# Two attention stages: values as the stationary operand in two column halves, probabilities divided on GpSimd, and one maximum over two banks

## The chip, the cores and the metric

The kernel runs on one core of a Trainium2 chip, as one launch. The metric is the time on the device in microseconds (us), the median over several runs. A core has TensorE (PE; its weight loads are PEld), VectorE (DVE), ScalarE (ACT), GpSimd (POOL) and the DMA queue of SyncE (SP). They run at the same time and wait for each other only through semaphores.

## The reference

The reference is a small language model block of three mixers over 512 tokens of width 1024, in fp32. The first is a hybrid layer. The second and third are a forgetting attention ("fox") and a latent attention ("mla"), each with 12 heads of 64, beside 4 heads that look at a memory of 256 tokens, and each followed by an output projection and a convolutional feed-forward block. What the change touches is the softmax attention of the second and third:

```python
logits = jnp.einsum('bhqd,bhkd->bhqk', qc, k).astype(jnp.float32)
if log_decay is not None:
    logits = logits + args[2][..., None] - log_decay[:, :, None, :]
logits = jnp.where(key_idx[None, :] <= q_idx[:, None], logits, -jnp.inf)
p = jax.nn.softmax(logits, axis=-1).astype(v.dtype)
return jnp.einsum('bhqk,bhkd->bhqd', p, v)
...
x = x + jnp.concatenate([o_mix, o_mem], axis=-1) @ w_out[i]
```

`log_decay` is there in forgetting attention only. The attention is causal, over query blocks of 128, so a head's block i has 128 (i + 1) keys. The memory heads have all 256 keys for every block and no mask.

## The kernel before

One list, `SCHEDULE` (made by `schedule()`, line 2893), fixes the order of all work. It names a stage for each step, and every engine's program walks through the same list; the engine's generator for that stage then issues what belongs to that step. So each engine's order is written by hand and served strictly in order; waits go by named events (`Signal`, `Waits`). Buffers come from rings: `take` waits until the last holder of the buffer was released. PSUM is 8 banks of 128 x 512 fp32.

The dense products (projections, feed-forward) split each fp32 factor into a high part and a rest, both of the type fp32r, and sum three products (`mm3`, lines 320 to 323). Weights come by DMA into `wstage`; ScalarE makes the high part (L302) and VectorE the rest (L312), in pieces set between the other steps.

Both attention stages use the class `Attention` and the generators `pe_att`, `act_att` and `dve_att` (lines 989 to 1222), as does the first mixer's banded attention. An item is one head and one block of 128 queries; with 16 heads there are 64 items in a mixer. Items come in pairs of heads. In forgetting attention the two heads of a pair alternate and their scores are made together, one head in each half of the array's rows (64 channels each); `fox_order` (L2230) sets a group of memory items between them. In latent attention a head has 96 channels, and a head's four blocks come one after another. At step t:

- TensorE makes the scores of item t (L1051 to L1068) in a bank, transposes the probabilities of item t - 3 (L1077), block by block of 128 keys, and multiplies those of item t - 5 with the values (L1092). There the transposed probabilities are the stationary operand (128 x 128) and the 64 columns of the values stream. The result is queries by channels, in a bank for both heads of a pair.
- VectorE takes the negated maximum of item t - 1 (L1182), and copies the transposed probabilities of item t - 3 out of their bank (L465), except those of forgetting attention's memory heads, which ScalarE copies (L460).
- ScalarE makes the exponential with the sum of its row (L1140). In latent attention it first multiplies the maximum by the query's norm, a column of 128 (L1138).
- Five and six steps after a pair's last item VectorE takes the reciprocals of the 8 sums (L1191) and multiplies the outputs of each block (L1197, four for a pair) into `y`. TensorE then transposes `y`, four blocks (L1108), and ScalarE and VectorE split the result into `hhi` and `hlo` (L418, L427), the operand of the output projection.

The output projection's first tile (`pe_out`, step 0) runs between the last steps of attention. In latent attention the projections of the heads to come (`pe_group`, `act_group`, `dve_group`, `pool_group`) share the first 43 steps.

```python
for t in A.steps:                       # pe_att, L1095
    if 0 <= t < N and A.scored(t) and not late:
        score(A.scored(t))
    if 3 <= t <= N + 2:
        turn(t - 3)
    if 5 <= t <= N + 4:
        pv(t - 5)
```

## Time and profile before

| what | value |
|---|---|
| median of 3 runs | 1573.14 us (1569.53 to 1573.67) |
| time of the profiled execution | 1568.96 us |
| span of the profiled execution | 1567.2 us |
| TensorE busy | 1532.4 us, 98% |
| VectorE busy | 824.6 us, 53% |
| ScalarE busy | 723.4 us, 46% |
| GpSimd busy | 317.8 us, 20% |
| mean granted TensorE clock | 0.998 |

The span goes from the first to the last instruction; the time of the execution is 1.8 us more. "Busy" counts an engine as busy while any of its instructions runs. The instructions of one engine overlap (a matmul's duration includes the time until its result has landed), so a count times a mean duration is more than the busy time, and what one instruction costs in a dense stretch is the distance between two starts.

### The profile page before, as it was taken

How to read it: one execution, taken by the hardware profiler on the slowest of the kernel's cores; microseconds unless marked ns; L12 is line 12 of the kernel's file. 1: busy time of each engine (PE TensorE's matmuls, PEld its weight loads, DVE VectorE, ACT ScalarE, POOL GpSimd, SP SyncE). 2: the span in 40 equal slices, each digit the busy share in tenths (PEclk: the TensorE clock that was granted, in tenths of full speed). 3: DMA queues.
4: the chain of work that ended last, by engine and by line, in shares of the span. 5: the costliest groups of instructions: out<-in, count | busy, mean ns of one | idle time of the engine just before them, and what ended most of it. 6: DMA issues, size and time to landing. Idle time of an engine off the chain costs nothing. (4 is left out here: it accounts for less than half of the span.)

```text
span 1567.2 us, 22136 instructions
## 1 busy us (share of the span) xinstructions
PE 1532.4 (98%) x9018; PEld 1288.9 (82%) x9018; DVE 824.6 (53%) x1405; ACT 723.4 (46%) x1402; POOL 317.8 (20%) x270
## 2 busy tenths in 40 slices
PE   7999998999999999999999999999999999999999
PEld 6888887998898887888888888668887888888887
DVE  5346556556435755745234443668956544244442
ACT  4346545455654544544124443567844443134431
POOL 0000142001430001344013431032001433024420
PEclk9999999999999999999999999999999999999999
DMA  6212112323220103233223332110022333223331
GB/s 234 75 41 88 54 55 89 129 68 108 78 89 27 39 1 108 82 107 119 90 79 102 100 111 75 48 44 14 16 66 81 105 97 122 80 81 98 114 111 41
DMA packets 37462, 128.07 MB, mean 82 GB/s; under 512 B 4192, under 2 KB 8944, under 8 KB 37360
## 3 DMA queue, kind: packets, MB, share of 16 engines
q1 hardware_dynamic: 37360, 126.65, 24.9%
q8 instruction: 71, 1.16, 0.3%
q14 instruction: 31, 0.25, 0.1%
HBM read 124.54 MB, written 2.10 MB: 81 GB/s over the span
## 5 line engine op out<-in xcount | busy, mean ns | idle before, releaser
L321 PE MATMUL bank<-hhi,whi 128*128 128x512 f32 (+2 forms) x1064 | 418.3, 393 | 2.8 <-ACT hhi L1936 1.8
L323 PE MATMUL bank<-hhi,wlo 128*128 128x512 f32 (+2 forms) x1064 | 414.4, 390 | 0.0
L322 PE MATMUL bank<-hlo,whi 128*128 128x512 f32 (+2 forms) x1064 | 414.2, 389 | 0.0
L312 DVE TENSOR_TENSOR wlo<-wstage,whi 128x1024 fp32r<-128x1024 f32 (+9 forms) x250 | 278.6, 1117 | 112.2 <-ACT whi L302 111.8
L302 ACT CAST whi<-wstage 128x1024 fp32r<-128x1024 f32 (+9 forms) x250 | 236.1, 949 | 135.6 <-PE bank L323 131.7
L2421 DVE SCALAR_TENSOR_TENSOR cr<-bank,vc,cr 128x511 f32<-128x511 f32 (+1 forms) x168 | 125.9, 749 | 217.1 <-ACT cr L2360 214.1
L321 PEld LDWEIGHTS bank<-hhi,whi 128*128 128x128 f32 (+2 forms) x1064 | 198.7, 187 | 49.3 <-ACT hhi L1936 4.3
L323 PEld LDWEIGHTS bank<-hhi,wlo 128*128 128x128 f32 (+2 forms) x1064 | 198.6, 187 | 43.2
L322 PEld LDWEIGHTS bank<-hlo,whi 128*128 128x128 f32 (+2 forms) x1064 | 198.7, 187 | 41.7 <-issue 0.5
L2360 ACT ACTIVATE cr<-bank,vc 128x512 f32<-128x512 f32 x84 | 65.5, 780 | 248.5 <-PE bank L323 246.1
L2466 POOL TENSOR_TENSOR cr<-cr,cr 128x512 f32<-128x512 f32 x44 | 94.4, 2146 | 315.4 <-DVE cr L2421 280.7
L321 PE MATMUL bank<-ahi,whi 128*128 128x512 f32 x352 | 137.8, 392 | 1.7 <-POOL alo L2472 1.7
L323 PE MATMUL bank<-ahi,wlo 128*128 128x512 f32 x352 | 137.1, 389 | 0.0
L322 PE MATMUL bank<-alo,whi 128*128 128x512 f32 x352 | 137.0, 389 | 0.0
L2472 POOL TENSOR_TENSOR alo<-cr,ahi 128x512 fp32r<-128x512 f32 x44 | 95.6, 2172 | 118.9 <-ACT ahi L2372 118.8
L321 PE MATMUL bank<-whi,hhi 128*128 128x384 f32 (+3 forms) x288 | 96.8, 336 | 1.5 <-issue 0.9
L322 PE MATMUL bank<-wlo,hhi 128*128 128x384 f32 (+3 forms) x288 | 94.1, 327 | 1.7 <-issue 1.7
L2445 DVE TENSOR_TENSOR xT<-bank,xT 128x512 f32<-128x512 f32 x32 | 22.1, 691 | 137.1 <-PE bank L323 137.1
L323 PE MATMUL bank<-whi,hlo 128*128 128x384 f32 (+3 forms) x288 | 94.1, 327 | 0.0
L321 PEld LDWEIGHTS bank<-ahi,whi 128*128 128x128 f32 x352 | 66.1, 188 | 16.7 <-issue 3.3
L323 PEld LDWEIGHTS bank<-ahi,wlo 128*128 128x128 f32 x352 | 66.1, 188 | 13.9
L322 PEld LDWEIGHTS bank<-alo,whi 128*128 128x128 f32 x352 | 66.1, 188 | 13.4
(412 smaller groups left out, 2298.5 us busy)
## 6 DMA issues: line engine op xcount, KB each, us to landing
wstage<-in_wts SPq DMA_DIRECT2D x147, 512.0 KB, 3.5
wstage<-in_wts SPq DMA_DIRECT2D x32, 704.0 KB, 4.0
wstage<-in_wts SPq DMA_DIRECT2D x14, 768.0 KB, 4.3
xT<-in_x SPq DMA_DIRECT2D x4, 512.0 KB, 5.3
xt<-in_x SPq DMA_DIRECT2D x4, 512.0 KB, 5.9
out<-ob SPq DMA_DIRECT2D x8, 256.0 KB, 2.3
U<-in_rel_ext SPq DMA_DIRECT2D x6, 256.0 KB, 9.0
wstage<-in_wts SPq DMA_DIRECT2D x2, 603.0 KB, 3.9
```

The source lines that it names most:

```text
L302: e.copy(K.whi[i % 3][:, p], K.stage[i % 3][:, p]).then_inc(*K.act.up(("whi", i, p.stop)))
L312: e.tensor_tensor(K.wlo[i % 3][:, p], K.stage[i % 3][:, p], K.whi[i % 3][:, p].bitcast(F32), SUB).then_inc(*K.dve.up(("wlo", i) if last el ...
L321: e.matmul(o, lh, rh, start=start, stop=False)
L322: e.matmul(o, lh, rl, start=False, stop=False)
L323: return e.matmul(o, ll, rh, start=False, stop=stop)
L2360: e.activation(t[:], divided(K, 1 + 2 * l, key) if first else K.bank(key)[:], ACT.Identity, scale=K.col(f"cw{l}", 3 * ch + 2), bias=K.col( ...
L2421: e.scalar_tensor_tensor(out=t[:, s:T], in0=b[:, 0:T - s], scalar=K.col(f"cw{l}", 3 * ch + 2 - s), in1=t[:, s:T], op0=MUL, op1=ADD).then_i ...
L2445: e.tensor_tensor(K.xT[:, m, :], K.bank((down, hv, m))[:], K.xT[:, m, :], ADD).then_inc(*K.dve.up(done, frees=[(down, hv, m)]))
L2466: e.tensor_tensor(g[:], g[:], v[:], MUL).then_inc(*K.pool.up(("gated", l, ch), frees=[((up, 22 + ch), "cr")]))
L2472: e.tensor_tensor(alo[:, ct, :], g[:], ahi[:, ct, :].bitcast(F32), SUB).then_inc(*K.pool.up(("alo", l, hv, ct), frees=[((up, 11 * hv + ct) ...
```

## The change

The first mixer keeps `pe_att`, `act_att` and `dve_att`, with their branches for the others removed. The other two get a subclass and generators of their own:

- The transposed probabilities are the streaming operand and the values (128 keys x 64 channels) the stationary one. The result comes out as channels by queries, the first head of a pair in partitions 0 to 63 and the second in 64 to 127 of one bank; `values(p, i)` issues the products of both heads for a block, alternating.
- The division by the sums comes before the transpose. For every two items VectorE takes the reciprocals (2 columns), and GpSimd multiplies the probabilities by them, in place, one instruction an item.
- `y`, its divisions (L1197) and its transposes (L1108) are gone; `hhi` and `hlo` are made from the bank of the products.
- The transpose of item t comes at step t + 5, the products of a block 7 steps after its second item; there are 7 buffers for probabilities in place of 5, and one buffer a head and block for the transposed ones.
- In forgetting attention one `tensor_reduce` takes the maxima of two items, from two adjacent banks (banks 0 to 3 are now one tensor).
- In latent attention the product of maximum and norm is GpSimd's.
- Banks are dealt out anew, and the steps of the schedule's lists change by one or two.

```diff
+class TurnedAttention(Attention):
+    TURN, VALUES = 5, 7
...
+def pe_turned(e, q, K, A):
...
     def turn(t):
         n = A.n(t)
         b = A.T.take(q, (A.name, "T", t))
-        q.wait_ge(*K.at((A.name, "P", t)))
+        q.wait_ge(*K.at((A.name, "divided", t)))
...
+    def values(p, i):
+        if i == 0:
+            (A.O4 if p < 2 else A.O).take(q, (A.name, "O", p))
+        for t, item in enumerate(A.items):
+            if item in ((2 * p, i), (2 * p + 1, i)):
+                q.wait_ge(*K.at((A.name, "pt", t)))
+        n = A.blocks(2 * p, i)
+        z = {}
+        for j in range(n):
...
+            for s in range(2):
+                o = K.bank((A.name, "O", p))[64 * s:64 * s + 64, i * P:(i + 1) * P]
+                z[s] = e.matmul(o, A.heads[2 * p + s].v(j), A.turned(p, i)[s][:, j, :], start=j == 0, stop=j == n - 1)
...
     for t in A.steps:
         late = 0 <= t < N and A.R is not None and A.items[t][0] >= 4
         if 0 <= t < N and A.scored(t) and not late:
             score(A.scored(t))
-        if 3 <= t <= N + 2:
-            turn(t - 3)
-        if 5 <= t <= N + 4:
-            pv(t - 5)
...
+        if t - A.VALUES in A.ends:
+            values(*A.ends[t - A.VALUES])
+        if 0 <= t - A.TURN < N:
+            turn(t - A.TURN)
...
+def act_turned(e, q, K, A):
...
-            e.activation(m, m, ACT.Identity, scale=factor).then_inc(*K.act.up((A.name, "mx", t)))
...
+        p = A.done(t - A.VALUES - 1)
         if p is not None:
             kt = (p + 6) % 8
-            act_hi(e, q, K, (A.gen, "hi", kt), (A.name, "yT", p), K.hhi[:, kt, :])
+            for i in range(4):
+                q.wait_ge(*K.at((A.name, "pv", p, i)))
+            e.copy(K.hhi[:, kt, :], K.bank((A.name, "O", p))[:]).then_inc(*K.act.up((A.gen, "hi", kt)))
...
+def dve_turned(e, q, K, A):
...
+    def soft_two(t):
+        h, i = A.items[t]
+        n, m = A.n(t), A.mx[:, h:h + 2, i]
+        q.wait_ge(*K.at((A.name, "S", t)))
+        q.wait_ge(*K.at((A.name, "S", t + 1)))
+        e.tensor_reduce(m, K.both[t % 4][:, :, 0:n], AX, MAX, negate=True).then_inc(*K.dve.up((A.name, "mx", t), (A.name, "mx", t + 1)))
...
+        u = t - 3
+        if 0 <= u < N and u % 2 == 0:
+            q.wait_ge(*K.at((A.name, "P", u)))
+            q.wait_ge(*K.at((A.name, "P", u + 1)))
+            e.reciprocal(A.sums(u), A.sums(u)).then_inc(*K.dve.up((A.name, "rr", u)))
...
+def pool_turned(e, q, K, A):
+    N = len(A.items)
+    for t in A.steps:
+        u = t - 1
+        if 0 <= u < N and A.heads[A.items[u][0]].factor:
...
+            e.tensor_tensor(m, m, factor, MUL).then_inc(*K.pool.up((A.name, "mx", u)))
+        u = t - 3
+        if 0 <= u < N and u % 2 == 0:
+            q.wait_ge(*K.at((A.name, "rr", u)))
+            for item in (u, u + 1):
+                h, i = A.items[item]
+                p = A.P[A.name, "P", item][:, 0:A.n(item)]
+                e.tensor_scalar(p, p, A.rs[:, h, i:i + 1], None, MUL).then_inc(*K.pool.up((A.name, "divided", item)))
...
-    out += ["fox", "foxatt", "foxatt"] * 5 + ["foxatt"] * 61
-    out += ["out0"] + ["foxatt"] * 3 + ["out0"] * 7 + ["bar5"] + ["norm1"] * 2 + ["ffn0"] * 63 + ["bar6"] + ["norm2"] * 2
+    out += ["fox", "foxatt", "foxatt"] * 5 + ["foxatt"] * 60
+    out += ["out0"] + ["foxatt"] * 5 + ["out0"] * 7 + ["bar5"] + ["norm1"] * 2 + ["ffn0"] * 63 + ["bar6"] + ["norm2"] * 2
```

## Rows read from the trace of the kernel before

**Rows 1.** The page: the span, and part 1, busy time of each engine.
```profile
span 1567.2 us, 22136 instructions
...
PE 1532.4 (98%) x9018; PEld 1288.9 (82%) x9018; DVE 824.6 (53%) x1405; ACT 723.4 (46%) x1402; POOL 317.8 (20%) x270
```

**Rows 2.** Windows: length, busy (instructions) of PE, PEld, DVE, ACT, POOL; clock; DMA.
```profile
484.00:573.00 89.00, 87.66 (x828) 76.78 (x827) 61.58 (x166) 48.67 (x161) 0.00 (x0) 1.00 0.06 19
1028.00:1066.00 38.00, 34.36 (x217) 27.19 (x216) 27.65 (x73) 28.22 (x91) 17.16 (x23) 0.96 0.12 36
1066.00:1151.00 85.00, 81.70 (x668) 73.82 (x667) 73.11 (x178) 67.36 (x196) 7.78 (x10) 1.00 0.08 26
```

**Rows 3.** Lines with each shape apart, TensorE, 482 to 574 us: busy, mean | idle.
```profile
L1092 PE MATMUL bank<-fv,fox_pt 128*128 128x64 f32 x240 | 31.9, 265 | 0.0
...
L1092 PE MATMUL bank<-vmem,fox_pta 128*128 128x64 f32 x64 | 8.9, 262 | 0.0
...
L1108 PE MATMUL bank<-ident,y 128*128 128x128 f32 x28 | 4.4, 279 | 0.3 <-DVE y L1197 0.3
```

**Rows 4.** The same view, TensorE, 1028 to 1154 us.
```profile
L1092 PE MATMUL bank<-vt,mla_pt 128*128 128x64 f32 x240 | 31.9, 265 | 0.0
...
L1092 PE MATMUL bank<-vmem,mla_pt 128*128 128x64 f32 x64 | 9.4, 271 | 2.0 <-DVE y L1197 2.0
```

**Rows 5.** Timeline, TensorE, 566 to 582 us: start, length, engine, line, count.
```profile
570.25 2.57 PE L1092 MATMUL bank<-fv,fox_pt 128*128 128x64 f32 x22
```

**Rows 6.** Lines with each shape apart, TensorE, the whole span: fp32 products of two widths.
```profile
L1884 PE MATMUL bank<-tmp,ones 128*128 128x512 f32 x6 | 3.1, 592 | 0.0
...
L2009 PE MATMUL bank<-tmp,blk 128*128 128x256 f32 x4 | 1.0, 380 | 0.0
```

**Rows 7.** Timelines, TensorE, from 540.1 and from 243.7 us: row halves, column strips.
```profile
540.20 0.70 PE L1051 MATMUL bank<-kmg,mqT 64*128 64x256 f32 x4
...
243.71 0.34 PE L1503 MATMUL bank<-gq,gk 32*32 32x32 f32 x32
```

**Rows 8.** Timeline, TensorE, 541 to 546.5 us.
```profile
541.61 0.60 PE L1077 MATMUL bank<-ident,tmp 128*128 128x128 f32 x4
...
543.27 0.23 PE L1068 MATMUL bank<-later,below 64*128 64x64 bf16 x4
543.43 0.66 PE L1077 MATMUL bank<-ident,tmp 128*128 128x128 f32 x4
...
544.77 1.00 PE L1092 MATMUL bank<-fv,fox_pt 128*128 128x64 f32 x8
545.70 0.39 PE L1051 MATMUL bank<-fkh,fqh 64*128 64x256 f32 x2
```

**Rows 9.** Lines with each shape apart, VectorE, 482 to 574 us.
```profile
L1182 DVE TENSOR_REDUCE fox_mx<-bank 128x1 f32<-128x512 f32 x12 | 8.2, 680 | 0.6 <-PE bank L1068 0.6
L1197 DVE TENSOR_TENSOR y<-bank,fox_rs 128x128 f32<-128x128 f32 x32 | 7.6, 282 | 0.3
...
L1182 DVE TENSOR_REDUCE fox_mx<-bank 128x1 f32<-128x128 f32 x12 | 3.0, 281 | 1.5 <-PE bank L1068 1.5
L1191 DVE RECIPROCAL fox_rs<-fox_rs 128x8 f32<-128x8 f32 x8 | 1.6, 202 | 13.1 <-PE bank L1092 13.1
```

**Rows 10.** Lines, ScalarE: one row of 1028 to 1154 us, two of 482 to 574.
```profile
L1138 ACT ACTIVATE mla_mx<-mla_mx,r 128x1 f32<-128x1 f32 x48 | 14.0, 292 | 14.3 <-DVE mla_mx L1182 14.2
...
L1140 ACT ACTIVATION_READ_ACCUMULATOR tmp<-bank,fox_mx 128x1 f32 x64 | 12.5, 196 | 0.0
L1140 ACT ACTIVATE tmp<-bank,fox_mx 128x512 f32<-128x512 f32 x12 | 8.3, 688 | 3.8 <-DVE fox_mx L1182 3.8
```

**Rows 11.** Lines with each shape apart, GpSimd, the whole span.
```profile
L2472 POOL TENSOR_TENSOR alo<-cr,ahi 128x512 fp32r<-128x512 f32 x44 | 95.6, 2172 | 118.9 <-ACT ahi L2372 118.8
...
L1871 POOL TENSOR_TENSOR sum<-sum,tmp 128x512 f32<-128x512 f32 x10 | 13.0, 1300 | 41.3 <-ACT tmp L1835 41.3
...
L2822 POOL COPY kt<-krr 128x512 f32<-128x512 f32 x3 | 1.8, 611 | 51.3 <-DVE krr L2703 51.2
```

More of the change, by code:

```diff
@@ L1042, in pe_att, with turned_to @@
+def turned_to(A, q, K, t):
+    h, i = A.items[t]
+    if A.before[h // 2, i] is not None:
+        q.wait_ge(*K.at((A.name, "pv", *A.before[h // 2, i])))
+    else:
+        for event in A.free_after:
+            q.wait_ge(*K.at(event))
+    n = A.blocks(h, i)
+    return A.turned(h // 2, i)[h % 2], K.bank((A.name, "T", t))[:, 0:n * P].rearrange("p (j n) -> p j n", j=n)
 def pe_att(e, q, K, A):
@@ L1047, in score @@
+def pe_turned(e, q, K, A):
+    N = len(A.items)
+    def score(ts):
+        at = [(t, A.items[t][1], A.heads[A.items[t][0]], A.n(t), A.scores(t).take(q, (A.name, "S", t))) for t in ts]
         z = {}
@@ L2853, in pool_group @@
             *K.pool.up(("k", j, "normed", h)))
-    yield
-    for _ in range(3):
         yield
```

313 lines of the change are left out of this document (194 added, 119 removed).

## The prediction

> **What bounds the kernel now.** I began with the page: TensorE is busy for 98% of the span and no other engine for more than 53% [rows 1]. So time goes only where TensorE's work shrinks, or where TensorE waits. Then I cut out the two stages that the change touches, by the windows view [rows 2]. In forgetting attention (484 to 573 us) TensorE is idle for 1.3 of 89 us, and VectorE is busy for 61.6. Latent attention has an early part that shares its time with the projections of its heads (1028 to 1066), and a late part (1066 to 1151) in which TensorE is idle for 3.3 of 85 us and VectorE busy for 73.1. So the first stage is TensorE's alone; in the second VectorE stands close behind. GpSimd does nothing in the first stage and 7.8 us in the late part of the second.
>
> **TensorE, the products with the values.** An fp32 product is two passes in the trace: 120 blocks of 128 by 128 show as 240, and each mixer has 240 + 64 = 304 passes [rows 3, 4]. A run of 22 passes lasts 2.57 us with its last 0.275 [rows 5], so they start 2.295/21 = 0.109 us apart. That is not the 64 columns that stream: a pass of 512 columns takes 0.592 us and one of 256 takes 0.380 [rows 6], 0.83 ns a column, so 64 columns are 0.05 us. What fills 0.109 us is the load of 128 columns of weights. After the change a pass loads 64 columns and streams 128: 128 x 0.83 = 0.106 us, with a load of half the width (about 0.05) that the earlier pass can cover. One pass is thus hardly cheaper. The gain hangs on the two heads running side by side in the two column halves. Two rows speak for it. The memory heads' scores use two row halves, and their four passes of 256 columns fit in 0.70 us [rows 7], where four in turn would need four times 256 x 0.83 = 0.85 us before any load. For columns, 32 passes of 32 by 32 run in 0.34 us, the last 0.19 of it, so all start within 0.15 us [rows 7]; with four row strips alone, one strip would stream eight passes of 32 x 0.83 = 0.027 us, 0.21 us. Passes in one strip but different column strips must have overlapped, and in fp32. So I take full overlap: 152 passes' time of 0.106 per mixer, 16.1 us, in place of 304 x 0.109 = 33.1. That is -17.0 per mixer. The bound on the other side is no overlap, 32.2 us.
>
> The Trainium skill (TensorE: Matmul & The Clock Gate, section "Measured speedup vs the span model") reports 2.38 for three column tiles, not 3. At that efficiency (0.79) the products would take an estimated 20.4 us a mixer and the sum would be 8.6 us smaller; no row here has halves of 64 columns.
>
> **TensorE, the rest.** The transposes of y go: 32 per mixer (28 before 574 us) [rows 3]; four of their size start (0.60 - 0.27)/3 = 0.11 us apart [rows 8], so -3.5 per mixer. A change of tile shape costs: the last product before a score starts at 544.77 + 1.00 - 0.275 = 545.50, the score at 545.70 [rows 8], 0.20 in place of 0.11; the way back (543.27 to 543.43) loses as much. I take 0.1 a change. In forgetting attention the order score, transpose, product becomes score, product, transpose, three changes in place of two for each of 32 calls of values(); in latent attention the scores span 96 rows and needed none, so each call adds two. With 0.05 for a first load in each call: +4.8 and +8.0. TensorE's sum: -17.0 - 3.5 + 4.8 = -15.7 in forgetting, -17.0 - 3.5 + 8.0 = -12.5 in latent attention. Of the latter the late part has 240 of 304 passes and 24 of 32 calls: -10.0; the early part -2.5.
>
> **VectorE.** The 32 divisions of y go, 0.282 each, 9.0 us; reciprocals go from 8 to 32 at 0.20, +4.8 [rows 9]. A maximum costs 0.281 for 128 and 0.680 for 512 columns [rows 9], so 0.15 fixed; 32 double ones in place of 64 save 4.8. (Never shown is one over two banks: from no saving to 0.15 each.) Busy in forgetting attention: 61.6 - 9.0 + 4.8 - 4.8 = 52.6, of a stage that TensorE needs 89 - 15.7 = 73.3 for: 72%, nearly its share now, so TensorE keeps its gain. In the late part of latent attention: 73.1 - 24 x 0.282 + 18 x 0.20 = 69.9, against TensorE's 85 - 10.0 = 75.0, or 93%, where it is 86% now. An engine that serves in order can't be that full without being waited for; I take 92%, 76 us, a gain of 9. In the early part the projections' norms set the pace (VectorE 27.7, ScalarE 28.2 and GpSimd 17.2 busy of 38): gain 1.
>
> **ScalarE** loses 48 scalings of 0.29 us, 14.0 us [rows 10], to GpSimd, which does them in the same chain (maximum, scaling, exponential): nothing saved on latency. It is not the bound; 0.
>
> **GpSimd** gets 128 divisions. Per mixer these are 6 pairs x 2 heads x 1280 columns + 16 x 256 = 19,456, or 38 full widths. The trace has none with one input and a scalar per row. Ends: a copy of 512 takes 0.611; a two-input operation 1.30, or 2.17 in the feed-forward stage [rows 11]. I take 0.65, next to the one-input row: 25 us a mixer, hidden beside TensorE, as 1.30 (49 us) would be too. What the division does add is length: the transpose comes at step t+5, not t+3. From the end of a 512-wide score pair: double maximum 1.2, two exponentials 0.69 each with their accumulator reads [rows 10], reciprocal 0.2, division 0.65; some 4 us against five steps of TensorE, 5 us. That holds in mid-stage. At the end nothing follows the last items, so transpose 62 waits about 2 us before the output projection's first tile; it then covers the last one. -2 for each mixer. The single output bank is freed by ScalarE's and VectorE's parts of y three or more steps before its next use, as a memory group stands between pairs: 0.
>
> **Sum.** Forgetting 15.7 - 2 = 13.7; latent 9 + 1 - 2 = 8; together 22. Against the profiled execution's 1568.96 us that is 1547. The median of the runs is 4.2 us higher, so 1551.
>
> **Rivals.** (1) VectorE keeps up all the same: TensorE's sum counts whole, 15.7 + 12.5 = 28, giving 1545. For: VectorE's buffers are several steps deep. Against: 93%. (2) GpSimd becomes the bound. At the feed-forward stage's 2.17 us a width, forgetting attention needs 38 x 2.17 = 82 us of it (gain 7) and the late part 30 x 2.17 + 7.8 + 48 small scalings of up to 0.29, 87 us, no gain: 1566. For: the same operation costs 1.30 or 2.17 by where it runs. Against: it has one input here, and VectorE's work beside it reads mostly the banks. The Trainium skill (GPSIMD Engine Reference, Specifications) says that the shared SBUF interfaces clash when VectorE has two SBUF inputs; by that rule forgetting attention, where only the weights' splits do, is free, and no run so far shows the divisions. (3) Slower: the halves take turns. Place: values(). If the loads stay hidden the products cost 64.4 in place of 66.3, -1.9, less 7.0 for y, plus 12.8 for changes and loads: +4. If a load can't pass the other half's stream, 608 x 0.05 = 30 more. So +4 to +34, 1577 to 1607, with 1590 as its time. It decides once a pass costs on average over 0.10 us (66.3 + 7.0 - 12.8 = 60.5 over 608), where I expect 0.053. Against it the 32 by 32 row; for it, both halves stream all 128 rows, which that row doesn't. (4) The edit does less than it says: probabilities arrive so late that TensorE's saved time becomes waiting for "divided" at each wide pair, 1 us x 12 in each mixer: 1573, no change.
>
> **Chances.** Forecast 0.60, (1) 0.13, (2) 0.10, (3) 0.12, (4) 0.05. A change of under 0.3% (4.7 us) can't be told from none here. Faster by more: 0.60 + 0.13 + most of (2), 0.82. Within: (4) and the top of (2), 0.06. Slower: 0.12. The range runs from just below (1), if the double maximum and the end chains cost nothing (1537), to (2) and the edge of (4), 1572; it leaves out (3) and half of (4).
>
> **What the changed profile would show.** Products of 128*64 with 128x128 in pairs that start within some ns, their pairs 0.11 us apart; forgetting attention about 75 us, the late part about 76; TensorE's idle there rising to some 5 us, put down to VectorE's copies or maxima; VectorE above 90%; divisions near 0.65 us. Wrong if the second half's passes start 0.1 us after the first's, if TensorE's waits name the division, or if GpSimd is busy for over half of a stage.

## The result, and the profile after

The change makes the kernel slower. Its median is 1614.16 us over 4 runs (1613.33 to 1619.62), beside 1571.34 us (1565.97 to 1573.67) for the kernel before: a ratio of 1.0285 with a 95% interval of 1.0248 to 1.0322. I had forecast 1551 us and a range up to 1572. The profiled execution took 1613.33 us, 44.4 more than that of before.

The page, the span and part 1:

```profile
span 1611.6 us, 22131 instructions
...
PE 1537.0 (95%) x8954; PEld 1264.4 (78%) x8954; DVE 816.8 (51%) x1357; ACT 706.9 (44%) x1354; POOL 458.1 (28%) x446
```

Beside [rows 1]: TensorE's busy time has not fallen at all, though it has less to do; GpSimd has 140.3 us more; VectorE and ScalarE have 7.8 and 16.5 less. To see where the 44.4 us lie I cut the span where both traces have the same event: the forgetting part runs from VectorE's first maximum to ScalarE's first activation of the feed-forward block, the latent part from the last activation of that block to the first of the next. These two rows, from the view of one tile (the feed-forward's, ScalarE), the first of before and the second of after, give one of these edges:

```profile
L2360 ACT ACTIVATE cr<-xd,vc x2: 802/808/815, 637.4 to 638.1; 128x512 f32<-128x512 f32 x2
```
```profile
L2529 ACT ACTIVATE cr<-xd,vc x2: 798/808/817, 651.7 to 652.4; 128x512 f32<-128x512 f32 x2
```

The first maximum starts at 482.2 and 482.3 us, so the forgetting part takes 155.2 us before and 169.4 after. The latent part takes 293.1 and 323.2. The feed-forward block between them (285.1) and all behind them (351.6) are the same within 0.1, here and in every run below. So +14.2 and +30.1, with 0.1 in the start, make the 44.4. The table holds these two lengths for all runs, as I read them off each trace, and beside each how long TensorE was granted the lower of its two clock levels in it (1.2 GHz; otherwise 2.4). Single runs are marked; their time stands for itself, without an interval. Ratios compare runs in the faster of two states; one of e18's four runs, at 1738.57 us, fell in the slower one and is left out.

| kernel | us | forgetting (half clock) | latent (half clock) |
|---|---|---|---|
| before | 1571 to 1573 | 155.2 (0) | 293.1 (3.4) |
| after | 1614.16 | 169.4 (13.7) | 323.2 (41.0) |
| e1_no_division, one run | 1586.75 | 155.5 (0) | 307.7 (27.3) |
| e2_half_columns, one run | 1600.53 | 163.2 (13.7) | 314.0 (41.0) |
| e3_vector_divides, one run | 1602.58 | 158.2 (3.4) | 319.9 (41.0) |
| e4_shared, one run | 1597.65 | 157.4 (3.4) | 317.5 (41.0) |
| e6_two_maxima_alone | 1573.14 | 157.2 (0) | 292.7 (3.4) |
| e14_scaling_alone | 1569.83 | 155.2 (0) | 292.2 (0) |
| e15_forgetting_alone, one run | 1584.82 | 171.6 (23.9) | 293.2 (3.4) |
| e7_scaling_on_scalar | 1610.67 | 170.8 (23.9) | 316.0 (34.1) |
| e9_single_maxima_scalar_scaling, one run | 1588.33 | 157.6 (6.8) | 309.5 (30.7) |
| e10_short, one run | 1578.07 | 148.6 (0) | 304.2 (23.9) |
| e11_filled, one run | 1611.62 | 167.1 (0) | 321.3 (27.3) |
| e12_fill_light, one run | 1568.46 | 148.6 (0) | 300.1 (10.2) |
| e13_even_values, one run | 1579.99 | 150.1 (3.4) | 305.0 (0) |
| e18_changed_filled_light | 1617.00 | 172.8 (27.3) | 321.4 (27.3) |
| e19_copies_on_scalar | 1574.02 | 155.2 (0) | 294.1 (3.4) |
| e20_filled_copies_on_scalar, one run | 1578.8 | 150.2 (3.4) | 305.2 (20.5) |
| e17_forgetting_shared | 1589.18 | 175.6 (30.7) | 291.8 (0) |

Some of this scatters without a change of code. The first maximum starts between 480.7 and 489.0 us over these profiles, though the work ahead of it is the same, and the ten runs of e6 spread over 8.9 us. So totals of single runs can't be compared to a few us; the parts are steadier. The latent attention of before stands in four profiles (before, e6, e15, e17) with 291.8 to 293.2 us. The forgetting attention of the changed kernel stands in four as well (after, e7, e15, e18) with 169.4, 170.8, 171.6 and 172.8, in the order of their time at half clock (13.7, 23.9, 23.9, 27.3).

The windows of the changed kernel: forgetting attention, its end beside the output projection's first tile, and latent attention's early and late part. The columns are those of [rows 2]:

```profile
482.00:575.00 93.00, 77.43 (x756) 55.42 (x756) 53.44 (x125) 44.64 (x159) 60.52 (x60) 0.96 0.06 18
575.00:592.00 17.00, 12.74 (x77) 9.54 (x75) 4.84 (x10) 1.93 (x5) 5.56 (x4) 0.80 0.00 0
1037.00:1075.00 38.00, 30.95 (x184) 21.72 (x183) 25.69 (x75) 26.77 (x88) 26.27 (x32) 0.95 0.15 46
1075.00:1187.00 112.00, 92.11 (x651) 71.98 (x649) 73.46 (x178) 58.41 (x162) 70.30 (x110) 0.86 0.05 15
```

TensorE now stands idle for 15.6 of 93 us and for 19.9 of 112, and works at a granted clock of 0.96 and 0.86. No engine is full: GpSimd, the busiest newcomer, reaches 65% and 63%. That is the picture of a chain of waits, not of a bound. The waits of 484 to 586 us and, in the second fence, of 1075 to 1187 us (who waited for whom, us in total, times, longest) name its links:

```profile
POOL tmp L1390 <- DVE fox_rs L1365: 45.6, 21, 22.0
DVE fox_pt L465 <- PE bank L1247: 24.7, 27, 3.0
...
PE bank L1247 <- POOL tmp L1390: 9.4, 7, 2.1
...
PE bank L1247 <- POOL fox_p L1390: 3.1, 2, 1.8
```
```profile
ACT tmp L1300 <- POOL mla_mx L1383: 34.7, 19, 3.3
...
ACT mla_p L1300 <- POOL mla_mx L1383: 15.1, 6, 5.5
...
PE bank L1247 <- POOL tmp L1390: 6.0, 7, 1.5
```

TensorE's transposes (L1247) wait for the division (L1390), the second of the three signs that I had named for a wrong forecast; GpSimd at 65% of the stage is the third. In latent attention ScalarE waits 49.8 us for the scaled maximum (L1383), which GpSimd serves in the same queue as the divisions.

### The profile page after: what moved, and what is told of

It reads as the page before. It is cut to its first block and busy times, and to the rows that moved or that the text cites. A ratio compares the mean times of both kernels' runs of the same rounds, so it can differ in the third digit from the quotient of the medians.

```text
span 1611.6 us, 22131 instructions
## 1 busy us (share of the span) xinstructions
PE 1537.0 (95%) x8954; PEld 1264.4 (78%) x8954; DVE 816.8 (51%) x1357; ACT 706.9 (44%) x1354; POOL 458.1 (28%) x446
## 5 line engine op out<-in xcount | busy, mean ns | idle before, releaser
L321 PE MATMUL bank0to<-hhi,whi 128*128 128x512 f32 x560 | 221.5, 396 | 2.8 <-ACT hhi L2105 1.8
L322 PE MATMUL bank0to<-hlo,whi 128*128 128x512 f32 x560 | 219.5, 392 | 0.0
L323 PE MATMUL bank0to<-hhi,wlo 128*128 128x512 f32 x560 | 219.3, 392 | 0.0
L321 PE MATMUL bank<-hhi,whi 128*128 128x512 f32 (+2 forms) x504 | 199.2, 395 | 0.0
L323 PE MATMUL bank<-hhi,wlo 128*128 128x512 f32 (+2 forms) x504 | 196.8, 391 | 0.0
L322 PE MATMUL bank<-hlo,whi 128*128 128x512 f32 (+2 forms) x504 | 196.7, 390 | 0.0
L321 PEld LDWEIGHTS bank0to<-hhi,whi 128*128 128x128 f32 x560 | 106.2, 190 | 28.5 <-ACT hhi L2105 4.2
L323 PEld LDWEIGHTS bank0to<-hhi,wlo 128*128 128x128 f32 x560 | 106.0, 189 | 22.5
L322 PEld LDWEIGHTS bank0to<-hlo,whi 128*128 128x128 f32 x560 | 106.1, 190 | 21.4
L323 PEld LDWEIGHTS bank<-hhi,wlo 128*128 128x128 f32 (+2 forms) x504 | 93.8, 186 | 21.4
```

Source lines behind the costliest of these rows:

```text
L321: e.matmul(o, lh, rh, start=start, stop=False)
L322: e.matmul(o, lh, rl, start=False, stop=False)
L323: return e.matmul(o, ll, rh, start=False, stop=stop)
```

## What the operations cost

The lines of GpSimd with each shape apart, 482 to 620 us, and behind them one row of the same view of ScalarE's old work, now GpSimd's (930 to 1200 us):

```profile
L1390 POOL TENSOR_SCALAR tmp<-tmp,fox_rs 128x256 f32<-128x256 f32 x19 | 17.4, 923 | 28.5 <-DVE fox_rs L1365 28.2
L1390 POOL TENSOR_SCALAR tmp<-tmp,fox_rs 128x512 f32<-128x512 f32 x10 | 15.5, 1563 | 2.3 <-DVE fox_rs L1365 2.3
L1390 POOL TENSOR_SCALAR tmp<-tmp,fox_rs 128x384 f32<-128x384 f32 x8 | 9.9, 1243 | 5.9 <-DVE fox_rs L1365 5.9
...
L1390 POOL TENSOR_SCALAR tmp<-tmp,fox_rs 128x128 f32<-128x128 f32 x9 | 5.3, 603 | 9.2 <-DVE fox_rs L1365 9.2
```
```profile
L1383 POOL TENSOR_TENSOR mla_mx<-mla_mx,r 128x1 f32<-128x1 f32 x48 | 8.7, 189 | 13.5 <-DVE mla_mx L1333 12.4 <-ACT mla_p L1300 1.0
```

A division costs 283 ns and 2.5 ns a column, so 1.563 us for 512 columns, where I had taken 0.65. (In latent attention the rows of the 512-wide ones average 1.59 and 1.66.) A mixer has 12 of each width and 16 more of 256: 12 x (0.603 + 0.923 + 1.243 + 1.563) + 16 x 0.923 = 66.8 us, where I had 25. The Trainium skill (GPSIMD Engine Reference, section 3.1) gives 1.8 cycles an element at 1.2 GHz as the best case of a tight loop, 0.77 us for 512, and about 2.6 for two inputs; these rows show 2.5 ns a column, which at that clock would be three cycles, for one input and a scalar per row. The measurement decides.

TensorE's own part came as forecast. Timeline of TensorE, 515 to 592 us:

```profile
524.80 1.09 PE L1265 MATMUL bank<-fox_pt,fv 128*64 128x128 f32 x16
...
538.63 1.55 PE L1265 MATMUL bank<-fox_pt,fv 128*64 128x128 f32 x12
...
588.73 0.88 PE L1265 MATMUL bank<-fox_pt,fv 128*64 128x128 f32 x12
```

Sixteen passes, eight in each column half, last 1.09 us. The single starts are 524.801 and 524.807, 524.961 and 524.967, then 525.070 and 525.077, and so on by 0.109: the halves run side by side, and a pair costs what one pass did [rows 5]. The middle row is the same work as the last, at half clock: 1.55 in place of 0.88 us.

## Where the chain comes from

One pair of 512 columns can be followed through the timeline of all engines, 559 to 568 us of the changed kernel:

```profile
559.30 0.23 PE L1238 MATMUL bank0to<-later,below 64*128 64x64 bf16 x4
...
560.62 1.22 DVE L1343 TENSOR_REDUCE fox_mx<-bank0to 128x2 f32<-128x1024 f32 x1
...
561.87 0.69 ACT L1300 ACTIVATE tmp<-bank0to,fox_mx 128x512 f32<-128x512 f32 x1 [1.75 <-DVE fox_mx L1343]
...
562.34 2.46 POOL L1390 TENSOR_SCALAR tmp<-tmp,fox_rs 128x384 f32<-128x384 f32 x2 [1.82 <-DVE fox_rs L1365]
...
562.55 0.68 ACT L1300 ACTIVATE tmp<-bank0to,fox_mx 128x512 f32<-128x512 f32 x1
...
563.73 0.52 PE L1247 MATMUL bank<-ident,tmp 128*128 128x128 f32 x3 [1.76 <-POOL tmp L1390]
...
564.28 0.56 DVE L465 COPY fox_pt<-bank 128x384 f32<-128x384 f32 x1 [1.12 <-PE bank L1247]
...
564.76 0.16 DVE L1365 RECIPROCAL fox_rs<-fox_rs 128x2 f32<-128x2 f32 x1
...
565.01 3.10 POOL L1390 TENSOR_SCALAR tmp<-tmp,fox_rs 128x512 f32<-128x512 f32 x2 [0.21 <-DVE fox_rs L1365]
```

The pair's scores end at 559.53, its maximum starts at 560.62, its exponentials end at 563.32 with their sums, and its second division ends at 568.11: 8.6 us, where I had "some 4 us". Three things make it long. The maximum starts 1.1 us after the scores, behind other work of VectorE. Both items' divisions count, 3.10 us, and I had counted one of 0.65. And 1.7 us pass between the sums and the first division. The reciprocal, ready to go at 563.32, starts at 564.76, because on VectorE it stands behind a copy that waits for TensorE's transpose of the pair before, which at 563.73 had waited 1.76 us for that pair's division on GpSimd. GpSimd itself is busy with that pair until 562.34 + 2.46 = 564.80, so for this pair a prompt reciprocal would have brought only 0.21 us; before the 384-wide divisions it was GpSimd that waited, 1.82 us. So the delay goes round: division, transpose, copy, reciprocal, next division, and GpSimd's own queue is a part of it.

## Experiments: the division

Two theories stood first: that the divisions make the loss, by their price and their place in the chain, or that the rest of the new order does (the longer pipeline, the places of the products, the clock), so that free divisions would not help. In e1 the divisions are left out and TensorE waits for the reciprocal in their place; the output is undivided.

```diff
-                e.tensor_scalar(p, p, A.rs[:, h, i:i + 1], None, MUL).then_inc(*K.pool.up((A.name, "divided", item)))
...
-        q.wait_ge(*K.at((A.name, "divided", t)))
+        q.wait_ge(*K.at((A.name, "rr", t - t % 2)))
```

> The changed kernel without GpSimd's 128 divisions; the transpose waits for the reciprocals in their place, so the result is left undivided, and all else stays. Theory A (GpSimd's division is the bound: 283 ns + 2.5 ns a column in the changed trace, 67 us a mixer): the time falls from 1614 to 1540 to 1555 us, the clock stays at 0.99 or more. Theory B (the longer way from score to transpose, two steps and a wait for pairs, costs by itself): it stays above 1580. Theory C (the column halves or the changes of shape cost): stays above 1590.

In e2 only the first half of each item's columns is divided.

```diff
-                p = A.P[A.name, "P", item][:, 0:A.n(item)]
+                p = A.P[A.name, "P", item][:, 0:A.n(item) // 2]
```

> The changed kernel with GpSimd dividing only the first half of each item's columns (the other half is left undivided). Theory A as throughput: GpSimd needs 64 x 0.28 + 9728 x 0.0025 = 42 us a mixer in place of 67, below TensorE's 73, so most of the loss goes: 1550 to 1575 us. Theory A as latency in the chain: about half of the way between the changed kernel and the one without divisions. Theory B or C: little change, above 1590.

Without divisions the two parts shrink by 13.9 and 15.5 us, 29.4 of the 44.3 lost; with half the columns by 6.2 and 9.2, 15.4, about half of that. e1's 1586.75 us lie far above theory A's 1540 to 1555 and within theory B's. In e2 the fixed 283 ns of a division stay, so GpSimd's divisions fall by over a third only, from 66.8 to an estimated 42.4 us, and yet the two parts gain 52% of what they gain without any division. e2's 1600.53 us lie about halfway between the changed kernel and e1, as I had put for a chain of waits, and not at 1550 to 1575, as I had put for throughput. So the cost follows the length of the division, though not in proportion to it. The divisions are two thirds of the loss; the rest, 0.3 us in forgetting and 14.6 in latent attention, is there without any division.

e3 gives all divisions to VectorE; e4 gives the first item of each two to VectorE and leaves the second to GpSimd.

```diff
             e.reciprocal(A.sums(u), A.sums(u)).then_inc(*K.dve.up((A.name, "rr", u)))
+            q.wait_ge(*K.at((A.name, "rr", u)))
+            for item in (u, u + 1):
...
+                e.tensor_scalar(p, p, A.rs[:, h, i:i + 1], None, MUL).then_inc(*K.dve.up((A.name, "divided", item)))
```

> The changed kernel with all 128 divisions on VectorE, behind its reciprocals. Theory A: forgetting attention gains (VectorE has room there), latent attention is bound by VectorE; 1560 to 1590 us in sum, depending on the price of a 512-wide division on VectorE, which no run has shown (0.3 to 0.7 us). Theory B: no gain over the changed kernel, about 1610.

> The changed kernel with the first item of each two divided by VectorE and the second by GpSimd. Theory A: GpSimd falls to 33 us a mixer and VectorE rises by 10 to 22; 1550 to 1575 us, below the kernel before if VectorE's part is short. Theory B: about 1600.

A row of each, the lines with each shape apart (VectorE in e3, GpSimd in e4, 482 to 600 us):

```profile
L1370 DVE TENSOR_SCALAR tmp<-tmp,fox_rs 128x512 f32<-128x512 f32 x10 | 4.5, 483 | 0.2
```
```profile
L1395 POOL TENSOR_SCALAR tmp<-tmp,fox_rs 128x512 f32<-128x512 f32 x5 | 9.3, 1861 | 4.9 <-DVE fox_rs L1365 4.9
```

VectorE divides 512 columns in 0.483 us, a third of GpSimd's time. It recovers 11.2 us of forgetting attention's 14.2, and only 3.3 of latent attention's 30.1; why so little there, no run shows. Shared is the lowest of the three (157.4 and 317.5). GpSimd needs 0.09, 0.16, 0.23 and 0.30 us more for 128 to 512 columns in it: each of its divisions starts 0.06 us after VectorE's of the same width, and the extra grows by 0.52 ns a column, as VectorE's own division does (0.284 to 0.483 us). e3 and e4 are both slower than the kernel before, and slower than I had put them (1560 to 1590, 1550 to 1575).

## Experiments: the parts of the change alone

e6 puts only the double maximum into the kernel before (banks 0 to 3 as one tensor, maxima of forgetting attention for two items at each odd step). e14 puts only the 48 scalings of the maxima on GpSimd there.

```diff
+            if late <= t < N + late and t % 2 == 1:
+                soft_two(t - 1)
```

> The kernel before with only the double maximum in forgetting attention (adjacent banks, 32 reductions for 64). Theory D (the double maximum makes both exponentials of a pair wait for the longer reduction, and the four banks of scores come free later): 3 to 12 us slower than the kernel before, the idle time of TensorE in 482 to 574 us rises from 1.3 us. Theory A or C (only the division or the halves matter): within 0.3% of before, VectorE's busy time down by some 4 us.

```diff
-            e.activation(m, m, ACT.Identity, scale=factor).then_inc(*K.act.up((A.name, "mx", t)))
...
+            e.tensor_tensor(m, m, factor, MUL).then_inc(*K.pool.up((A.name, "mx", u)))
```

> The kernel before with only one part of the change: latent attention's 48 scalings on GpSimd (0.19 us each there, 0.29 on ScalarE). Theory H (latent attention's even pace of 6.5 us a head was VectorE's and ScalarE's, not TensorE's): its time moves by over 2 us, down if ScalarE's 14 us count, up if the way by a third engine does. If TensorE paced it: within 0.3% of before.

Neither moves the time: 1.0002 (0.9985 to 1.0019) and 0.9996 (0.9984 to 1.0007). e6's profile does have 2.0 us more in forgetting attention, all of it behind the last maximum; its interval reaches 3 us and can't exclude that, but it excludes most of the 3 to 12 of theory D. A maximum over 2 x 512 scores takes 1.220 us in e6, two single ones would take 1.360 [rows 9], so the saving is what I took it to be, 0.14. TensorE is busy for 87.66 of 89 us there [rows 2], and it buys nothing.

e15 has the changed forgetting attention and the latent attention of before.

```diff
-        "mlaatt": lambda: pe_turned(e, q, K, K.mlaatt), "group0": lambda: pe_group(e, q, K, 0, K.RH),
+        "mlaatt": lambda: pe_old(e, q, K, K.mlaatt), "group0": lambda: pe_group(e, q, K, 0, K.RH),
```

> The change in forgetting attention alone, latent attention as before. The loss is additive by stages if this runs at 1583 to 1590 us (14 us of the 44 belonged to forgetting attention) and latent attention takes 293 us again.

The latent part is back at 293.2 and the forgetting part keeps its loss (171.6): the two losses are separate and add. That forgetting attention has 23.9 us at half clock here and 13.7 in the changed kernel, with the same code, shows that the clock's share scatters from run to run, here by 10 us, with 2.2 us in the length of the part.

e7 is the changed kernel with the scaling back on ScalarE; e9 is e1 with that and with single maxima.

```diff
-            e.tensor_tensor(m, m, factor, MUL).then_inc(*K.pool.up((A.name, "mx", u)))
...
+            e.activation(m, m, ACT.Identity, scale=factor).then_inc(*K.act.up((A.name, "mx", t)))
```

> The changed kernel with the 48 scalings of latent attention on ScalarE again; the divisions stay on GpSimd. Theory J (on GpSimd a scaling queues behind divisions of up to 1.6 us and a head's norms, and ScalarE's exponential waits for it: 51 us of such waits in the changed trace): latent attention falls by 8 us or more from 323.2 us. Theory A as latency of the division alone (TensorE's transposes wait for it whatever else GpSimd does): it falls by under 3 us. Without divisions the place of the scalings made no difference (307.7 and 309.5 us).

> The changed kernel without divisions (1586.8 us), with a maximum for each item again in forgetting attention and the 48 scalings of latent attention on ScalarE again. The stages tell the two apart. Theory D: forgetting attention (first maximum to first feed-forward activation, 155.5 us without divisions, 155.2 before) falls to 145 us or less. Theory E (the way by GpSimd between maximum and exponential is the longer one, and ScalarE waits for it): latent attention falls by 5 us or more from 307.6 us. Theory B (length of the pipeline): neither falls by over 3 us.

e7 gives 1.0250 (1.0228 to 1.0271). In its profile the latent part is 7.2 us shorter than in the changed kernel, and the forgetting part 1.4 longer. So the 49.8 us of ScalarE's waits (34.7 and 15.1, above) were worth some 7 on the path, between the 8 or more of theory J and the under 3 of theory A: a small operation that was moved into the queue of long ones. This rests on one profile of each, with 6.9 us less at half clock; the whole time fell by 3.5 us, and its interval overlaps that of the changed kernel. Without divisions the same move is worth nothing (e9 309.5, e1 307.7), so it would be what the scaling queues behind, and not its place. Single maxima bring nothing either: forgetting attention takes 157.6 us in e9 and 155.5 in e1, where theory D had 145.

## Experiments: the length of the pipeline

e10 is without divisions, like e1, and transposes 3 steps behind the item and multiplies 5 behind, as the kernel before.

```diff
-    TURN, VALUES = 5, 7
+    TURN, VALUES = 3, 5
...
-        q.wait_ge(*K.at((A.name, "divided", t)))
+        q.wait_ge(*K.at((A.name, "P", t)))
```

> The changed kernel without divisions, with the transpose at step t + 3 waiting for the exponential alone and the products 5 steps behind, as before the change. Theory B (two more steps and the wait for pairs are what is left of the loss): 1586.8 falls to 1550 us or below. Theory D or E (the waits lie between score and exponential, ahead of the transpose): it stays within 8 us of 1586.8.

The edit also lets a transpose wait for its own exponential and no longer for the reciprocal of its pair. The parts shrink by 6.9 and 3.5 us against e1; its 1578.07 us lie between the 1550 of theory B and the range of D and E. In forgetting attention this is a gain over before at last, 148.6 against 155.2. But TensorE's busy time fell by more. The windows of forgetting attention to the feed-forward block, before and e10:

```profile
482.00:637.20 155.20, 152.57 (x1111) 129.16 (x1110) 98.58 (x219) 77.18 (x202) 7.80 (x6) 1.00 0.13 42
```
```profile
487.00:635.00 148.00, 140.29 (x1076) 106.58 (x1075) 90.65 (x178) 74.45 (x202) 7.80 (x6) 1.00 0.14 44
```

TensorE does 12.3 us less (I had forecast 15.7), VectorE 7.9 less (9.0). Of these 12.3 us, 6.6 shorten the part and the rest is idle time, 7.7 us in place of 2.6 (the second window is 0.6 us shorter than the part). So even with free divisions TensorE would not have kept its gain. One wait that has grown, before (484 to 573 us) and in e10 (484 to 580), is that of the scores' first product for ScalarE's exponentials, which free the scores' banks:

```profile
PEld bank L1051 <- ACT tmp L1140: 0.7, 4, 0.2
```
```profile
PEld bank0to L1221 <- ACT tmp L1300: 5.2, 14, 1.0
```

e11 is e1 with every product issued twice.

```diff
-        for j in range(n):
+        for j in [*range(n), *range(n)]:
```

> The changed kernel without divisions, with every product with the values issued twice (the second run starts the sum anew, so the result is the same): 304 more passes in pairs for each mixer, 16 us of TensorE at 2.4 GHz. Theory F (TensorE's clock falls to 1.2 GHz in latent attention because it now works too little, and that is what makes the stage slow): the granted clock of the stage returns to 1.00 and the time stays or falls, 1575 to 1587 us. Theory D or E (waits alone, the clock follows from them): the clock rises but the time rises too or stays, 1587 to 1605.

The 16 us of passes a mixer that this adds cost 11.6 us in forgetting and 13.6 in latent attention, 24.9 in all, although TensorE had idle time in both. The time at half clock in the latent part stays at 27.3 us, as in e1, so theory F fell in this form. The products are on the path: as the next section shows for latent attention, their steps are the dense ones, and the idle time lies in other steps.

## Experiments: dense and light heads

In latent attention an item's partner, the same block of the other head, comes four items later. The products of both are issued together, so they all fall into the four steps behind the second head's items, and the steps of the other head have none. The windows of e10, four heads of latent attention, a dense and a light one, then a light and a dense one, and of before, two heads:

```profile
1109.80:1119.80 10.00, 9.94 (x72) 8.21 (x73) 6.06 (x15) 5.95 (x18) 1.03 (x6) 0.70 0.00 0
1119.80:1126.80 7.00, 5.32 (x41) 4.32 (x40) 6.14 (x15) 4.35 (x12) 0.77 (x4) 0.95 0.00 1
1135.00:1142.00 7.00, 5.32 (x43) 4.31 (x42) 6.14 (x15) 4.34 (x12) 0.77 (x4) 1.00 0.00 0
1142.00:1148.50 6.50, 6.50 (x68) 5.28 (x67) 5.54 (x15) 4.79 (x14) 0.76 (x4) 1.00 0.27 83
```
```profile
1122.20:1128.60 6.40, 6.40 (x58) 5.88 (x57) 6.02 (x15) 5.23 (x17) 0.00 (x0) 1.00 0.26 83
1128.60:1135.60 7.00, 6.83 (x59) 6.17 (x58) 6.29 (x17) 6.26 (x19) 0.00 (x0) 1.00 0.01 2
```

Before, both heads of a pair load TensorE alike (58 and 59 products and scores) and it is full in both: 13.23 us of 13.40. In e10 it does 5.32 + 6.50 = 11.82, 1.4 less. But the dense head (x68) fills it again, 6.50 of 6.50, and in the light one (x43) it stands idle for 1.68 of 7.00. All of the saving lies in the light head, which is as long as the same head of before, 7.00 us. And where the clock falls in a light head, the dense one behind it begins at 1.2 GHz: the first row, 9.94 us busy at a granted clock of 0.70 for 72 instructions, where 68 take 6.50 at 1.00. In the light head of the second row the clock falls 0.7 us before its end, at 1126.1 us. It does not fall in every light head; that of the third row, just as idle, and the dense one behind it have 1.00. So I had two theories for latent attention's 11 us: the clock that falls in light heads, and the dense heads themselves.

e12 is e10 with filler: in the light steps of the 12 latent heads the first score product is issued three times in place of once (the first two are overwritten).

```diff
+            for _ in range(2 if H.prep and t - A.VALUES not in A.ends else 0):
+                e.matmul(b[:, 0:n], H.q(i), H.k(n), start=True, stop=True)
             z[t] = e.matmul(b[:, 0:n], H.q(i), H.k(n), start=True, stop=not (H.causal or H.low or H.add or H.tri))
```

> The short pipeline without divisions (1578 us; latent attention 304.2 us with 24 us at half clock, 293.1 before), and in the 24 steps of latent attention's heads in which no product with the values falls due TensorE makes the first product of the scores three times (each begins the sum anew; 48 products more, some 7 us of work). Theory F (products bunched in four steps of eight leave TensorE light in between, the clock falls to 1.2 GHz there, and the dense steps then run at half speed): half clock shrinks to under 7 us, and latent attention falls by 4 us or more although it has more to do. Theory G (the stage is paced by the waits of VectorE and ScalarE, the clock costs nothing of its own): latent attention stays or rises by up to 7 us.

With the useless work the latent part takes 300.1 us in place of 304.2, and half clock 10.2 in place of 23.9; theory F had put 4 us or more and under 7 us at half clock. The windows of its heads 12 and 13:

```profile
1121.80:1128.40 6.60, 6.60 (x69) 5.37 (x68) 5.64 (x15) 5.03 (x15) 0.76 (x4) 1.00 0.26 79
1128.40:1135.50 7.10, 6.62 (x52) 5.60 (x51) 6.22 (x16) 4.44 (x12) 0.76 (x4) 1.00 0.01 2
```

The light head (the second) is as long as without filler, 7.03 between the first maxima of two heads in both. So it had room for 1.3 us of TensorE's work. But these are one run each. From the first maximum of the heads to the last they differ by 1.1 us only, and 2.9 lie behind it, where no filler is and where e10 has 6.9 us at half clock. And e20, below, has the same filler and 20.5 us at half clock. So that filler lifts the clock fits these traces and is not shown. The Trainium skill (TensorE: Matmul & The Clock Gate, "HAM oscillation") tells of a kernel whose waits for DMA send TensorE back to the lower clock again and again. e10's windows of 0.70 and 1.00 show such falls too, though with waits for other engines. With both parts at 448.7 us against 448.3, e12, which leaves out the divisions, is about level with the kernel before. Its 1568.46 us, one run, lie within the runs of the kernel before that were made beside it (1568.04 to 1574.09, median 1572.37).

e18 puts the same filler into the whole changed kernel, divisions and all.

> The changed kernel as it is (divisions on GpSimd and all), and in the 24 steps of latent attention's heads in which no product with the values falls due TensorE makes the first product of the scores three times: 48 products, some 7 us of work that nothing needs. Theory F (of the 30 us lost in latent attention the clock's fall is a part of its own, 41 us at half clock): half clock there under 20 us, and the kernel 5 to 15 us faster than the changed one, 1600 to 1609 us. Theory G (waits alone, the clock follows): as slow as the changed kernel or up to 7 us slower, 1614 to 1621.

Its ratio is 1.0288 (1.0268 to 1.0309), that of the changed kernel without it 1.0285. Half clock in the latent part falls from 41.0 to 27.3 us and the part only from 323.2 to 321.4. Theory F had put the kernel 5 to 15 us below the changed one. With the divisions in place the lower clock seems to cost little; that it lies where TensorE would otherwise wait is my reading, and no run shows it.

e13 is e10 with latent attention's products spread evenly: each head's at its own steps, the column halves one after the other, and two banks each for results and scores in place of the new deal.

```diff
+    def one(t):
+        h, i = A.items[t]
+        p, s = h // 2, h % 2
...
+            z = e.matmul(o, A.heads[h].v(j), A.turned(p, i)[s][:, j, :], start=j == 0, stop=j == n - 1)
```

> The short pipeline without divisions, and in latent attention each head's products at its own item's step, so that the halves take turns (32 us of passes in place of 16), with two banks for outputs and two for scores as before the change. Theory F (bunching and the clock): half clock back to 0 to 7 us and latent attention at 288 to 296 us, although TensorE has 16 us more to do. Theory G: latent attention at 304 us or above.

The windows of four of its heads, and a row of TensorE's timeline:

```profile
1114.30:1145.10 30.80, 30.80 (x219) 23.38 (x218) 24.11 (x59) 19.36 (x53) 3.03 (x16) 1.00 0.05 18
```
```profile
1135.68 1.09 PE L1281 MATMUL bank<-mla_pt,vt 128*64 128x128 f32 x8
```

The clock is full throughout the latent part, and yet it takes 305.0 us: theory F's 288 to 296 are missed. TensorE is full too, 30.80 of 30.80, at 7.70 us a head where before had 6.70. Eight passes now take the 1.09 us in which sixteen ran side by side. Against before, a pair of heads costs 15.40 - 13.23 = 2.17 us more although the four transposes of y (0.44) are gone; its passes are as many and as long, 0.109 apart. What is left are 8 calls: (2.17 + 0.44)/8 = 0.33 us a call, an estimate of what I had put at 0.25 (two changes of shape and a first load), if nothing else in TensorE's work differs. By the same sum the real change saves 20 x 0.109 + 0.44 - 4 x 0.33 = 1.3 us a pair; the windows of e10 show 1.4.

## Experiments: what paces latent attention

At full clock and with TensorE relieved, two heads still take 13.5 us. One theory (H) was that VectorE's copies of the transposed probabilities set this pace, as VectorE is busy for 6.14 of the light head's 7.00 us. e19 is e14 with the 24 copies of the first two blocks of each latent head on ScalarE; e20 is e12 with the same (the diff is that of e20).

```diff
-        return self.items[t][0] < self.on_act
+        h, i = self.items[t]
+        return h < self.on_act or self.R is not None and h >= 4 and i < 2
```

> The kernel before with the 48 scalings on GpSimd (no change by itself, ratio 0.9996) and, in the room that this gives ScalarE, the 24 copies of transposed probabilities of latent attention's blocks 0 and 1 on ScalarE. Theory H (VectorE paced latent attention at 6.5 us a head; 24 copies of 0.28 and 0.42 are 8.4 us of it): latent attention's heads fall from 87 to 79 to 84 us, the kernel by 3 to 7 us. If TensorE paced it: no change.

> The short pipeline without divisions and with the filled light steps (1568.5 us; latent attention 300.1 us, its heads 94.1), and the 24 copies of transposed probabilities of blocks 0 and 1 there on ScalarE in place of VectorE. Theory H (with less work on TensorE, VectorE sets the pace of latent attention, so the halves gain nothing there): VectorE loses 24 copies of 0.28 and 0.42, 8.4 us, and the heads fall by 3 us or more. If TensorE or the order of waits still sets it: within 1.5 us.

e19 changes nothing, 1.0005 (0.9990 to 1.0021). e20 is 5.1 us longer in the latent part than e12, one run each; half clock rose there from 10.2 to 20.5 us, but its light heads, at full clock, take 7.20 us in place of 7.03. Where theory H had 3 us or more less, both show none. Neither ScalarE's scalings (e14) nor these copies of VectorE set the pace. Which order of waits does, stays open.

## A version that wins?

e17 takes what was best in forgetting attention, shares its divisions as e4 does, shortens the pipeline by one step, and leaves latent attention as it was.

```diff
-    TURN, VALUES = 5, 7
+    TURN, VALUES = 4, 6
```

> The change in forgetting attention alone, with the division shared (VectorE the first item of two, GpSimd the second) and a pipeline of 4 and 6 steps in place of 5 and 7; latent attention as before. Without divisions a pipeline of 3 and 5 steps gave 148.6 us for the stage (155.2 before), shared divisions at 5 and 7 steps 157.4. Theory A with B (price and length of the division are all that is against the halves there): 150 to 155 us, the kernel 0 to 5 us below the one before. If the wait for the division decides at any length: 155 to 160 us, no gain.

Its ratio to before is 1.0105 (1.0089 to 1.0120), so it is about 1% slower, and its forgetting part, 175.6 us, is the longest of all, where I had expected 150 to 155. Two rows of its waits, 484 to 590 us:

```profile
PEld bank L1247 <- DVE tmp L1370: 15.8, 14, 2.9
...
PE bank L1247 <- DVE tmp L1370: 13.9, 15, 2.7
```

Once the transpose asks a step earlier, it waits for VectorE's division, and the half clock comes with it, 30.7 us. e4, with the same sharing and one step more, takes 157.4 us with 3.4 at half clock. So the steps that e10 could do without serve the division. I found no version that beats the kernel before.

## Why the prediction was wrong

**The sum for TensorE held.** Side by side in fp32: shown, 0.109 us for a pair, so -16.5 us a mixer (152 x 0.109 in place of 304 x 0.109; forecast -17.0); rival (3), halves in turn, did not happen. The shape changes were a little dearer (about 0.33 us a call by e13, not 0.25). In sum TensorE has 12.3 us less in forgetting attention (forecast 15.7) and 1.4 a pair of heads in latent attention, an estimated 10 in all with the memory heads (12.5). The efficiency of 0.79 that I set against it from the Trainium skill did not show for two halves.

**The step that failed first** is "I take 0.65 [...] 25 us a mixer, hidden beside TensorE, as 1.30 (49 us) would be too". The size was off by 2.4, though 1.563 lies inside my bounds. Worse was the reasoning: I compared a sum of busy time with the length of the stage. GpSimd is not full at 65%, and yet its divisions cost 29 us (e1), less when they are shorter (e2). It is not rival (2) either, for a bound would be full. The clash over SBUF that I named beside it does not show in the divisions of forgetting attention (1.563 us). In e4 GpSimd's divisions do take longer (1.861), but beside an operation of VectorE with one input and a scalar, which I had not counted as one that clashes.

**"Some 4 us against five steps of TensorE, 5 us; that holds in mid-stage"** is where that should have shown. The measured chain is 8.6 us: the second item's division was left out, and so were the queues: VectorE's, in which the maximum and the reciprocal stand, and GpSimd's own. Rival (4) named this mechanism and its wait, "divided", but priced it as giving back the gain and no more, at a chance of 0.05. As it came, the wait also delayed VectorE's copies, and more time at the lower clock came with it.

**"TensorE keeps its gain"** in forgetting attention failed as well: with free divisions and the short pipeline 6.6 of 12.3 us come back (e10). VectorE at 61% of that part is no bound. The scores wait 5.2 us for exponentials there, 0.7 before, so the scores, maxima and exponentials may form a loop of their own; no run isolates it.

**"92%, 76 us, a gain of 9"** in the late part took TensorE's load as even over the heads. It isn't: the products of a pair fall into one head, which is full (6.50 of 6.50), and the saving falls into the other, which it cannot shorten. Without divisions the part is still 11.1 us longer than before (e10), of which 4.1 are gone in the run with filler (e12). Of the other 7, 3.4 lie in one dense head that begins at half clock (9.8 us, 6.5 before), and 3.7 in the heads up to the one that starts at 1089.7 us, beside the projections, at as much half clock as before. Why those are longer is not settled. VectorE, for which I had put over 90% of the late part, is busy for 73.46 of 112 us in the changed kernel.

**The clock** is no term of my sum at all. The kernel before has 3.4 us at half clock in these parts, the changed one 54.7. Where the clock falls, the work behind is slower (1.55 in place of 0.88 us for the same twelve passes). What that cost in sum is open: the four profiles of the changed forgetting attention differ by 13.6 us at half clock and 3.4 in length, and e18 had 13.7 us less at half clock in latent attention and gained 1.8.

**ScalarE 0** was wrong for the scaling: "nothing saved on latency" left out that it queues behind divisions, some 7 us (e7, one profile of each). **"-2 for each mixer" at the ends** had the wrong sign. From its last maximum to the feed-forward block forgetting attention takes 77.0 us after the change, 72.8 without divisions, 69.5 to 71.1 with the short pipeline too, and 69.3 before: the longer pipeline and the divisions stick out at the end, where no items follow to cover them.

## What to carry to other kernels

Cost an operation that is put between two engines as latency, in the queue where it stands and with everything that its releaser queues behind, and only then as throughput; an engine at 65% can set the pace of all. Before you relieve the engine that is full, look how its load lies over the steps: a saving in steps that something else paces is idle time, and the clock can fall in it and be low in the steps behind. And a short operation should not be moved into the queue of long ones, however idle that engine is on average.

## What the runs showed of the hardware

- fp32 matmuls in the two column halves run fully side by side: the pairs start 6 to 7 ns apart and 0.109 us after one another.
- GpSimd's multiplication by a scalar per row takes 0.603, 0.923, 1.243 and 1.563 us for 128 to 512 columns, and 0.697 to 1.861 when VectorE does the same beside it (e4). VectorE takes 0.284 to 0.483 (e3). The two started 0.06 us apart, and GpSimd's extra grows with the columns as VectorE's own time does.
- TensorE's granted clock fell to 1.2 GHz at the end of a head in which it idled for 1.7 of 7 us (e10), but not behind another with the same idle time. Two runs with useless products in such heads had 10.2 and 20.5 us at half clock (e12, e20), beside 23.9 without (e10).
- One maximum over 1024 columns in two adjacent banks takes 1.220 us on VectorE, two of 512 take 1.360 (e6, [rows 9]).
